# Weight-sum steps spread over other tiles, and one low part computed ahead of a weight tile's, in a one-core hybrid decoder step

## What is computed

```python
h = rmsnorm(x, g_mix); z = h @ w_in                      # gates, retention q,k,v,g, RWKV r,k,v,loras
o_ret = head_norm(retention(rope(q), rope(k), v)) * silu(g_ret)
o_rwkv = (head_norm(rwkv7_scan(r, decay, k, v, -kk, kk * a)) ... + bonus) * g
x = x + (gate_a * (o_ret @ w_branch_a) + gate_b * (o_rwkv @ w_branch_b)) @ w_out
hq = rmsnorm(x, g_cross)
x = x + softmax((hq @ w_cq) @ mem_k.T / 16) @ mem_v @ w_co   # 4 heads, 256 memory tokens
hm = rmsnorm(x, g_mlp)
x = x + square(relu(hm @ w_up)) @ w_down                 # hidden 4096
y = rmsnorm(x, g_final)
```

## Time and profile before

| | us |
|---|---|
| median of three runs | 2244.88 (2243.84 to 2247.35) |
| profiled execution | 2245.65 |
| its span | 2243.7 |
| PE busy | 2165.4 (97%) |
| DVE busy | 1201.1 (54%) |
| ACT busy | 553.0 (25%) |
| POOL busy | 528.0 (24%) |

### The profile page before, as it was taken

How to read it: one execution, slowest core, us unless ns; L and a number is a source line. 1 busy time by engine, 2 the same in 40 slices (tenths; PEclk the granted TensorE clock), 3 DMA queues, 4 the chain that set the end, 5 groups by cost and what they waited for, 6 DMA issues and landing times. The chain is left out here.

```text
span 2243.7 us, 50369 instructions
## 1 busy us (share of the span) xinstructions
PE 2165.4 (97%) x21706; PEld 2039.3 (91%) x21706; DVE 1201.1 (54%) x1716; ACT 553.0 (25%) x1026; POOL 528.0 (24%) x444
## 2 busy tenths in 40 slices
PE   8999999999999899999999999999999999999997
PEld 6899888888888798979999998899999999999997
DVE  5433643636436327353544226349396875867865
ACT  3211433424333221144211014214021121121123
POOL 0233301203022032112344420222132221222220
PEclk9999999999999999999999999999999999999999
DMA  8346512617146278136335555212122222222222
GB/s 306 140 133 133 137 48 76 133 60 176 48 122 108 35 184 252 54 128 225 135 94 93 198 94 188 94 47 72 57 85 85 89 84 85 83 85 86 85 81 80
DMA packets 111500, 252.28 MB, mean 112 GB/s; under 512 B 11936, under 2 KB 49184, under 8 KB 108448
## 3 DMA queue, kind: packets, MB, share of 16 engines
q1 hardware_dynamic: 72736, 165.66, 22.3%
q0 software_dynamic: 27840, 58.72, 13.2%
q10 hardware_dynamic: 10752, 25.35, 3.2%
HBM read 221.64 MB, written 86.77 MB: 137 GB/s over the span
## 5 line engine op out<-in xcount | busy, mean ns | idle before, releaser
L564 PE MATMUL ps<-A_s,w_split 128*128 128x364 f32 (+1 forms) x3888 | 699.5, 335 | 3.8 <-ACT zstg L2424 3.8
L564 PEld LDWEIGHTS ps<-A_s,w_split 128*128 128x128 f32 x3888 | 647.6, 189 | 31.7 <-issue 14.4
L564 PE MATMUL ps<-hid,msp 128*128 128x272 f32 (+4 forms) x2592 | 357.5, 299 | 11.2 <-DVE hid L1529 10.8
L564 PEld LDWEIGHTS ps<-hid,msp 128*128 128x128 f32 x2592 | 351.7, 189 | 16.2 <-issue 10.3
L479 POOL CAST w_split<-w_raw 128x1024 fp32r<-128x1024 f32 x78 | 88.0, 1128 | 953.6 <-issue 472.8
L556 POOL CAST msp<-mraw 128x512 fp32r<-128x512 f32 x212 | 163.7, 773 | 542.7 <-PE ps L564 530.0
L564 PE MATMUL ps<-B_s,w_split 128*128 128x364 f32 (+1 forms) x1728 | 288.2, 328 | 0.7 <-POOL w_split L481 0.7
L564 PEld LDWEIGHTS ps<-B_s,w_split 128*128 128x128 f32 x1728 | 286.7, 188 | 1.0 <-issue 1.0
L481 POOL TENSOR_TENSOR w_split<-w_raw,w_split 128x1024 fp32r<-128x1024 f32 x78 | 205.5, 2635 | 6.3
L564 PE MATMUL ps<-xb,msp 128*128 128x272 f32 x1536 | 200.2, 288 | 1.4 <-DVE F L1529 1.4
L564 PEld LDWEIGHTS ps<-xb,msp 128*128 128x128 f32 x1536 | 195.7, 188 | 1.6 <-issue 1.6
(11 more groups left out here) (260 smaller groups left out, 2561.5 us busy)
## 6 DMA issues: line engine op xcount, KB each, us to landing
w_raw<-w SPq DMA_DIRECT2D x80, 512.0 KB, 3.7
mraw<-w SPq DMA_DIRECT2D x100, 256.0 KB, 2.7
sums_up<-w POOLq DMA_DIRECT2D x24, 1024.0 KB, 9.3
mraw<-sums_up SPq DMA_DIRECT2D x64, 256.0 KB, 2.6
z<-zstg SPq DMA_DIRECT2D x83, 182.0 KB, 2.5
sums_down<-w POOLq DMA_DIRECT2D x28, 512.0 KB, 7.8
mraw<-sums_down SPq DMA_DIRECT2D x48, 256.0 KB, 3.0
F<-z SPq DMA_DIRECT2D x16, 546.0 KB, 7.3
```

The lines of the kernel that those rows point to most:

```text
L564: return pe.matmul(out, lhsT, rhs, start=start, stop=stop, skip_group_check=skip)
```

## The change

The loop over tiles issues the weight-sum steps at other tiles: one per tile instead of two at tiles 21 to 33, one per tile from 54 to 71, and two per tile from 72. The number of steps and their order stay. In `down_fast`, the addition into `tf` and `lower(1, 1)` are both done in step 3, ahead of the low part of that step's weight tile; before, the addition stood behind it and `lower(1, 1)` at the end of step 4.

```diff
@@ -536,7 +536,7 @@
             done = 0
             for n in range(S_MLP - S_PW):
                 split(n, n % 2)
-                for _ in range(1 if n < 21 else 2 if n < 34 else 0 if n < S_OUT - S_PW else min(1, 64 - done)):
+                for _ in range(1 if n < 34 else 0 if n < S_OUT - S_PW else 1 if n < S_CQ - S_PW + 10 else min(2, 64 - done)):
                     if done < 32:
                         sum_step(done, 0, sum_block, up_block)
                     else:
@@ -2334,17 +2334,16 @@
                     read(p, 2 * u)
                     v.wait_ge(m_used, mlp_units(i, o, l + 1))
                     read(p, 2 * u + 1)
+                    if s == 3:
+                        v.wait_ge(m_lo, mlp_lows(i, o, d, 5))
+                        own.add(tt(tf, H22, tf, ALU.add))
+                        own.wait()
+                        lower(1, 1)
                     unit_lo(i, o, l + 4)
                     if s == 0:
                         turned_lo(H12, 0, 1, mlp_turns(i, o, d, 4, BEFORE_R + 5))
                     if s == 2:
                         turned_lo(tf, 0, 0, mlp_turns(i, o, d, 4, BEFORE_R + 6))
-                    if s == 3:
-                        v.wait_ge(m_lo, mlp_lows(i, o, d, 5))
-                        own.add(tt(tf, H22, tf, ALU.add))
-                    if s == 4:
-                        own.wait()
-                        lower(1, 1)
                     if s == 5:
                         own.add(tt(H21_hi, f32(hid[1][:, :, 0, 0:HT]), tf, ALU.subtract))
                     if s == 6:
```

## The result

The changed kernel takes 2280.37 us (median of four runs, 2276.25 to 2284.47) against 2244.36 us before on the same chip; the ratio is 1.0164 (95% interval 1.0134 to 1.0194). The forecast was 2278 in a range of 2258 to 2294. The profiled execution took 2282.57 us, its span is 2280.2.

What follows compares the result with a forecast made beforehand. TensorE, busy 2165.4 of 2243.7 us, was taken as the bound, so its added waits are paid in full. Losses 5.8 + 37.5 + 4.5 = 47.8 less gains 9 + 6 = 15 gave net 32.8 us, so 2278 us, range 2258 to 2294.

Steps and rivals of the forecast that it cites:

- What holds GpSimd: GpSimd's DMA queue: lets one accumulating transfer in as the one before is done, 8.2 us each, GpSimd standing still meanwhile.
- The rival by which it would keep up (2230): Tiles 71 to 77: accumulations under about 4 us fit beside the products, only gains stay, 2230 us; chance 0.06.
- estimate of 3.2 us for 512 KB: GpSimd's transfers: the skill page's fit, by which three would fit into a tile; the prediction went by the trace instead.
- Attention output tiles: Tiles 70 to 77: loss 37.5 us, about 17 as late splits and 20 as a wait for the last sum.
- Query tiles: Tiles 60 to 67: splits 65 and 66 late by 1.4 and 4.4 us, loss 5.8 us.
- Clock: TensorE after three long waits: half clock costs 1.5 us each, loss 4.5 us, bounds 0 and 9.
- Recurrence: Tiles 21 to 33: fewer TensorE "issue" waits, read as instruction fetch held up by weight-sum transfers; gain 9 us, bounds 0 and 14.
- The wait at 431: TensorE's "issue" wait in the recurrence, expected to stay because a 1 MB accumulation remains close ahead of it.
- Rival (b): Recurrence wins nothing because its waits come from elsewhere: 2287 us; chance 0.17.
- Low part: `down_fast` step 3: shorter VectorE chain before TensorE's product 3, 1.0 us in each of six, gain 6 us, bounds 4.5 and 8.
- the order against the weight tile's low part: `down_fast` step 3: `tf` and `lower` ahead of it shorten the chain by one low part and one read, 1.25 us.
- The sum: Whole kernel: losses 47.8, gains 15, net 32.8 us slower, 2278 us; chance 0.65.

Runs made afterwards that it cites:

- Experiment 4: Changed kernel with the twelve accumulating transfers of weight-sum steps 52 to 63 made plain copies (sums wrong): 2242.52 us in one run.
- Experiment 5: Changed kernel with GpSimd's DMA queue memory 2432 bytes instead of 2048: 2234.41 us, ratio 0.998 to the kernel before.
- Experiment 3: Changed kernel with weight-sum steps 0 to 46 at tiles 0 to 33 as before, none at 34 to 66, late tiles as changed: 2275.43 us, one run.
- experiment 6: Changed kernel with ScalarE's first loads of sample keys and values moved to the attention's start: 2272.96 us, ratio 1.0145 to the kernel before.
- Experiment 7: Changed kernel with no weight-sum step at tiles 21 to 33, two per tile at 34 to 44, then one: 2265.80 us, ratio 1.0114.
- experiment 1: Changed kernel's step 3 of `down_fast`, with weight-sum steps at the tiles of before: 2231.88 us, ratio 0.9964 to the kernel before.
- experiment 2: Weight-sum steps at the tiles of before; in step 3 the weight tile's low part first, then `tf` and `lower(1, 1)`: 2235.01 us, ratio 0.998.
- experiment 9: Changed kernel with weight-sum steps one per tile at 0 to 33, two at 40 to 43, one at 44, 45 and 49 to 68: 2223.28 us, ratio 0.9928.

## Why the prediction was right

**What holds GpSimd: right.** One accumulating transfer at a time, 8.2 us apart. In the attention's output they stand 7.7 to 8.5 us apart, wherever a second is wanted early. Experiments 4 and 5 show that it is room in the queue. The rival by which it would keep up (2230) falls: the gaps stayed, although the stage had little other traffic. The prediction's estimate of 3.2 us for 512 KB goes by the fit of the Trainium skill, page "DMA: Bandwidth & Descriptors", section "Anatomy of one DMA — SWDGE (gpsimd) path". No such transfer of GpSimd met it in any of these traces: accumulating ones landed after 7.3 us at least, plain copies after 4.2.

**Attention output tiles: right, to 1 us.** From the first transfer of tile 72 to the first MLP product the prediction has 1552.9 - 1436.6 = 116.3 us; measured 1557.04 - 1440.81 = 116.2. The stage lost 38.2 us against 37.5. The single waits were predicted as 2.3, 12.7, 2.4 and about 20 us and are 2.33, 10.65, 1.76 and 17.77, together 5 us less: tiles 73 and 77 ran slower and so used up 1.7 us each of the wait behind them, and the transfers came 8.0 to 8.1 us apart on average instead of 8.2. Experiment 3, where these two tiles ran at full clock, has the predicted waits: 2.14, 12.47, 2.05 and 19.51.

**Query tiles: mechanism right, size wrong.** Predicted 5.8 us; measured 12.3 us of waits, and 17.1 us for the stage. The step that failed is "with 8.2 us a transfer": one of these transfers let the next in only after 17.4 us, 9.2 more, and 5.8 + 9.2 = 15.0 is what tile 66 is late: it begins at 1284.53 where three tiles of 12.0 us after 1233.06 would have put it at 1269.1, 15.5 us. The row of landings gave its own warning, a longest of 18.4 us, and I took the median for all. The slow one stands beside four 1 MB loads of ScalarE, and with two of these moved away its landing fell from 17.2 to 11.6 us (experiment 6). Before, that slow transfer (1235.90) was followed only by copies, so nobody waited for it.

**Clock: right where it counts.** I took 1.5 us for each of the three long waits, 4.5 in all. Against 12.0 us a tile, the products behind these three took 1.6 us more (tiles 66 to 69), 1.5 (tiles 74 to 76) and 1.9 (the first MLP products, 8.08 instead of 6.19), 5.0 in all. Three more places ran slower that I had not counted: tile 64 by 2.7 us, tiles 73 and 77 by 1.7 each, with all six 11 us, above my bound of 9. But each of these three stands ahead of another wait for GpSimd or for the last sum and only shortens it. That they cost nothing was not foreseen. The granted clock in the 3 us behind the waits of 2.33, 10.65 and 1.84 us, in this order, 0.50 being 1.2 GHz and 1.00 2.4 GHz:

```profile
1462.00:1465.00 3.00, 3.00 (x11) 3.00 (x12) 3.00 (x4) 1.75 (x2) 0.00 (x0) 0.52 0.94 192
1486.30:1489.30 3.00, 3.00 (x10) 3.00 (x11) 0.00 (x0) 0.00 (x0) 2.46 (x4) 0.50 1.09 210
1268.30:1271.30 3.00, 3.00 (x18) 3.00 (x19) 0.00 (x0) 0.00 (x0) 0.01 (x1) 1.00 0.90 198
```

(columns as in the earlier trace rows). All waits over 4 us on split tiles in the changed kernel were followed by slower products. Of those of about 2 us some were and some not: 2.33 and 1.76 us were (tiles of 13.73 us), 1.84 us was not (12.21), nor were 2.14 and 2.05 in experiment 3 (12.18 and 12.23). The prediction already has both kinds; what makes the difference the runs do not show.

**Recurrence: right cause, gain in the upper half.** Predicted 9 us (0 to 14), measured 13.7 up to the first query tile in this pair of traces and about 12 on average of three and three. Experiment 7 shows that the transfers cause the waits, which in the prediction was only read from neighbourhood; the fetch of instructions stays unshown. The wait at 431 went too (0.2 us are left), though I had kept it. Rival (b), no gain there, is out.

**Low part: right.** Predicted 6 us and waits on `hid` of about 5; measured 5.2 us for the MLP in the changed kernel, whose first products run at half clock, so 7 without that, and 6.9 in experiment 1. The waits on `hid` all but vanished and 0.8 us on `F` took their place, 4.6 us in six places: TensorE now waits for the read of step 4, the next thing in VectorE's order. I kept 1.0 us for each down product; it is 1.15, between that and the full 1.25. I credited the order against the weight tile's low part; experiment 2 shows that it does not matter.

**The sum.** Predicted 47.8 - 15 = 32.8, measured 36.4 in the profiles. Losses were 17.1 + 38.2 = 55.3 instead of 47.8; the 7.5 us more are the one slow transfer (9.2), less what the other terms were over. Gains were 13.7 + 5.2 = 18.9 instead of 15, and some of that is the scatter of the first mark. Both sides were short, and the errors offset in part: that the time came within 2.4 us of 2278 is partly luck, the place and kind of the losses is not.

## What to carry to other kernels

An instruction that issues a DMA looks cheap, but the engine that issues it can be held for room in the queue; read the gap between two issues with no semaphore between them, multiply it by the longest run of such issues in the new order, and compare with the slack of what the same engine must do next. Moving background work out of a crowded stage pays only if the new place has long pieces of work to hide it and ends well ahead of the first reader. Use the slowest row of a group, not its median, where the new place is the one that made it slow. And where an engine runs behind another's fixed series of work, do not add its own slower clock to the lag: it is paid only where that engine is not waiting again right after.

## What was not expected of the hardware

Adding 384 bytes to GpSimd's DMA queue memory (2048 to 2432) moved the changed kernel from 1.6% slower than before to 0.2% faster. An accumulating DRAM-to-DRAM transfer of 512 KB let no second one in at 2048, and a plain copy of 1 MB did not either (experiment 9), while three plain copies of 512 KB were issued in 2.27 us. And 1.76 us of waiting between dense tiles was followed by a tile 1.7 us longer, while waits of 1.84 us (the changed kernel), 2.14 and 2.05 us (experiment 3) between tiles of the same shape, and one of 2.18 us in the MLP, were not followed by a lower clock; the runs do not show what makes the difference.
